# Pool branch by token in plain fp32 beside a modulation summed column by column

## The chip, the cores and the metric

The kernel runs on one core of one Trainium2 chip. The metric is the device time of one execution in microseconds (us). Its engines are TensorE (PE; its weight loads are PEld), VectorE (DVE), ScalarE (ACT), GpSimd (POOL) and SyncE (SP), which issues nearly all transfers. They run beside each other and are held together by semaphores only.

## The reference

Three blocks work on `x`, 256 tokens by 2048 channels. Only the first is touched, and of it the modulation and the first half of the pooling mixer:

```python
m = jnp.dot(jax.nn.silu(c), w) + b              # c: 2048, w: 2048 x 6144
shift, scale, gate = jnp.split(m, 3, axis=-1)
h = rms_norm(x) * (1.0 + scale) + shift
u, g = jnp.split(h @ w_in, 2, axis=-1)          # w_in: 2048 x 4096
# four groups of 512 channels, windows 2, 4, 8, 16
pooled = stack([centred_window_mean(ug[:, :, i], w) - ug[:, :, i] for i, w in enumerate(POOL_WINDOWS)])
y = einsum('btgc,gcd->btgd', pooled, w_grp).reshape(B, T, BRANCH_W) * scale_p
x = x + gate * ((y * silu(g)) @ w_out)
```

A gated deltanet block (A), an attention block (B) and a last norm follow. The program reads 290 MB of weights once. Since `pooled` is a difference of means over tokens, the shift, which is the same at every token, drops out of it; only `g` needs it.

## The kernel before

**Split products.** Nearly all weights come as *pieces* of 128 x 1024 floats (512 KB, two tiles of 128 rows of k by 512 columns; the code calls one a slab) through `raw`, a ring of 4 slots. ACT rounds a piece into `w_hi` (`hi_parts`, L912), DVE takes the rest into `w_lo` (`lo_parts`, L1204), both rings of 8 slots, and PE makes three fp32r products for each tile of k and each 128 channels (`by_channel`, L539, L541, L542), so 24 matmuls of 256 columns for a slab. The operand is split the same way, into `a_hi` and `a_lo` or `b_hi` and `b_lo`. Eight slabs make a `group` of 512 output channels. The groups of the pool block are u and g of four channel groups (0 to 7, 64 slabs), `w_grp` (8 slabs) and `w_out` (32 slabs). SP refills a slot of `raw` when the lo part, or the gate sum, of the piece before it is done (`piece`, L354). The waiting is in the order of the program.

**Modulation.** 32 transfers of 1 MB (`mod_ring`, 6 slots) hold 128 rows of k each of the shift and then the scale part of `w_mod`. DVE adds them up, each times a column of `silu_c`, into `mod_acc` (L1242, L1246), and PE sums `mod_acc` over the partitions (`mod_sums`, L589). The gate part comes as every third piece of the stream of u and g; DVE adds it (`add_gate`, L1183), and PE sums it after group 7.

**Norm.** ACT squares `x`, DVE adds the squares, PE sums them (`partition_sums`, L579), and ACT makes the root `r1` (L930, L932). DVE and ACT then make `a_hi` and `a_lo` (L1230, L921, L1214).

**Pooling.** DVE makes the window sums of each channel group by shifted adds (L1226, L1297), with ACT's copy of u as their input (L961).

The order within an engine is the order of the code. Everything from the group `w_grp` on is the same work before and after, with other line numbers.

Of the kernel before, what the change touches and what calls it, by code (L numbers as in the profile page):

```python
# [53 lines left out]
O_H, O_POOLED, O_Z = KT, KT + 4, KT + 8  # L54
# [9 lines left out]
V_C, V_BMOD, V_PSC, V_FG, V_NW0, V_NW1, V_CONV = 0, 16, 64, 80, 96, 112, 128  # L64
V_ONW, V_QNW, V_KNW, V_ALOG, V_DTB, V_EDGE, V_END = 320, 321, 322, 323, 339, 355, 419
# [69 lines left out]
def program(nc, weights, mod_w, x_t, vecs_d, consts_d, w_ab_d, bias_d, out_d):  # L135
    ctx = ExitStack()
    with ctx:
# [35 lines left out]
        r1 = at("r1", [P, T], F32)  # L173
# [3 lines left out]
        silu_c = at("silu_c", [P, KT], F32)  # L177
# [13 lines left out]

        mod_acc = at("mod_acc", [P, D], F32, t34_at)
# [63 lines left out]
        s_mod = [sem(f"s_mod{i}") for i in range(MOD_SLOTS)]  # L256
        s_mod_used = sem("s_mod_used")
        s_mod_sum = sem("s_mod_sum")
        s_vec = sem("s_vec")
        s_con = sem("s_con")  # L260
        s_x = sem("s_x")
        s_shift = sem("s_shift")
# [6 lines left out]
        s_act_read = sem("s_act_read")  # L269
        s_x1 = sem("s_x1")  # L270
        s_eps = sem("s_eps")
        s_pads = sem("s_pads")
# [72 lines left out]
        def _(sp):  # L345
            sp.dma_start(vecs[:], vecs_d).then_inc(s_vec, 16)
            for i in range(2 * KT):
                if i >= MOD_SLOTS:
                    sp.wait_ge(s_mod_used, i - MOD_SLOTS + 1)
                sp.dma_start(mod_ring[:, i % MOD_SLOTS], mod_w[i]).then_inc(s_mod[i % MOD_SLOTS], 16)  # L350
                if i == 1:
                    sp.dma_start(xres[:], x_t).then_inc(s_x, 16)

            def piece(q, slot, var=None, mul=0):  # L354


                before = q - RAW_SLOTS
                if before >= 0 or var is not None:
                    if before % 3 == 2:
                        sp.wait_ge(s_gate, Num(before // 3 + 1, var, mul // 3).v)  # L360
                    else:
                        sp.wait_ge(s_lo, Num(before // 3 * 2 + before % 3 + 1, var, mul // 3 * 2).v)
                land(Num(q, var, mul), slot)

            def land(q, slot):
                sp.dma_start(raw[:, slot], weights[bass.ds(q.times(P).v, P), :]).then_inc(s_raw[slot], 16)

            for q in range(12):
                piece(q, q % RAW_SLOTS)
            with sp.Fori(1, 8) as i:  # L370
                for q in range(12):
                    piece(q, q % RAW_SLOTS, i, 12)
            for q in range(12 * 8, 12 * 8 + 4):
                piece(q, q % RAW_SLOTS)
# [9 lines left out]
            slabs_between(N_GRP + 4, middle)  # L384
# [19 lines left out]
        def _(pool):  # L404
# [4 lines left out]
            pool.memset(t0[:], 0.0).then_inc(s_pads, 1)  # L409
# [122 lines left out]
        def _(pe):  # L532
# [51 lines left out]
            def mod_sums(pieces):  # L584

                for m in range(KT):

                    col = 512 * (m // (KT // pieces)) + m
                    last = nc.tensor.matmul(misc[:, col:col + 1], mod_acc[:, m * P:(m + 1) * P],  # L589
                                            ones[:, 0:1], start=True, stop=True)  # L590
                    if (m + 1) % (KT // pieces) == 0:
                        last.then_inc(s_mod_sum, 1)

            pe.wait_ge(s_con, 16)
            pe.wait_ge(s_sums, 1)
            partition_sums(t0, misc[:, 0:T])
            pe.wait_ge(s_mod_used, KT)
            pe.wait_ge(s_root, 1)
            mod_sums(1)
            pe.wait_ge(s_mod_used, 2 * KT)  # L600
            pe.wait_ge(s_shift, 1)
            mod_sums(4)


            group(None, Num(0), 0, 0, a_hi, a_lo, ready=lambda kt: kt + 1)
            group(None, Num(SLABS), 1, 0, a_hi, a_lo)
            with pe.Fori(1, 4) as i:
                for k in range(2):
                    group(Num(k - 1, i, 2), Num(k * SLABS, i, 2 * SLABS), k, 0, a_hi, a_lo)

            pe.wait_ge(s_gate, GATES)
            mod_sums(1)
            for j in range(4):
                group(Num(G_GRP + j - 1), Num(N_GRP + j * GRP_SLABS), j % 2, j * GRP_SLABS, b_hi, b_lo,
                      kt0=4 * j, slabs=GRP_SLABS, ready=lambda kt: O_H + j + 1)
# [8 lines left out]
            for j in range(4):  # L624
                g = Num(G_WOUT + j)
                group(g + (-1), slab_of(g), j % 2, N_WOUT % HL_SLOTS, a_hi, a_lo,
                      ready=lambda kt: O_POOLED + kt // 4 + 1, fillers={6: early_sums} if j == 3 else None)
# [270 lines left out]
        def _(act):  # L898
# [40 lines left out]
            for j, t in enumerate((t0, t1, t2, t1)):  # L939
                if j == 3:  # L940
                    act.wait_ge(s_dve, 1)
# [749 lines left out]
```

## Time and profile before

| | us |
|---|---|
| time, median of 3 runs (1568.35 to 1570.14) | 1568.76 |
| the profiled execution's own time | 1570.54 |
| its span | 1568.7 |
| PE busy | 1430.3 (91%) |
| DVE busy | 960.5 (61%) |
| ACT busy | 756.4 (48%) |
| moved by DMA | 302.56 MB, mean 193 GB/s |

Times within the profile are counted from the start of the span. A matmul's modelled end overlaps the next one's start: what one costs is the distance between two starts, not its "mean ns". The releaser of an idle stretch stands behind "<-".

### The profile page before, as it was taken

Reading aid. Unit: us, or ns where it says so; the run is one execution under the profiler, and the core shown is the slowest. Engines: PE = TensorE matmul, PEld = TensorE weight load, DVE = VectorE, ACT = ScalarE, POOL = GpSimd, SP = SyncE. Lnnn points to the kernel's source line nnn. Section 1 sums busy time; section 2 is a strip of 40 time slices with the busy share of each in tenths; the row PEclk is TensorE's granted clock in tenths of the full one; section 3 lists DMA queues with packets and bytes.
Section 4 is the critical chain, followed back from the end, with each engine's and each line's share of the span. In section 5 each row is a group of like instructions: output and inputs, shape, how many; then the busy total and the mean of one; then the engine's idle time right before and its main releaser. Section 6 shows DMA issues by size and latency. Waiting matters only on the chain.

```text
span 1568.7 us, 27728 instructions
## 1 busy us (share of the span) xinstructions
PE 1430.3 (91%) x11070; PEld 1398.6 (89%) x11070; DVE 960.5 (61%) x1092; ACT 756.4 (48%) x856; POOL 121.6 (8%) x128
## 2 busy tenths in 40 slices
PE   0149999999999999999959999999999999999998
PEld 0149999999999899899959999999999899998998
DVE  6798777776555666658863544674555655556542
ACT  2024444445557556573333555644656646556431
POOL 0000000000010212202033430000000000000000
PEclk9999999899999999999969999999999999999999
DMA  9977877765445444456474446655555655554562
GB/s 397 394 264 256 287 271 261 234 208 180 156 147 176 153 162 140 152 168 196 122 208 147 143 140 176 230 165 171 188 175 162 192 170 180 180 161 160 177 187 82
DMA packets 85500, 302.56 MB, mean 193 GB/s; under 512 B 17264, under 2 KB 17392, under 8 KB 80944
## 3 DMA queue, kind: packets, MB, share of 16 engines
q1 hardware_dynamic: 79584, 278.12, 53.7%
q0 software_dynamic: 5840, 23.33, 4.6%
q8 instruction: 59, 0.97, 0.3%
q14 instruction: 17, 0.14, 0.0%
HBM read 289.88 MB, written 13.63 MB: 193 GB/s over the span
## 4 chain that ended last, share of the span: by engine, by line
PE 46%; DVE 4%; ACT 1%; DMA 1%; issue 1%; SPq 0%; DVEq 0%; ACTq 0%
PE acc L539 11%; PE acc L541 11%; PE acc L542 11%; PE misc L737 2%; PE acc L550 2%; PE acc L552 2%; PE acc L551 2%; DVE w_lo L1204 1%; DVE t L1415 1%; DMA raw<-weights 1%; PE misc L854 0%; PE misc L788 0%; PE misc L831 0%; DVE prod L1226 0%; DVE inv L1226 0%
## 5 line engine op out<-in xcount | busy, mean ns | idle before, releaser
L1204 DVE TENSOR_TENSOR w_lo<-raw,w_hi 128x1024 fp32r<-128x1024 f32 x424 | 515.3, 1235 | 385.2 <-ACT w_hi L912 383.8
L912 ACT ACTIVATE w_hi<-raw 128x1024 fp32r<-128x1024 f32 x424 | 437.6, 1053 | 420.9 <-DMA raw<-weights 205.0
L539 PE MATMUL acc<-b_hi,w_hi 128*128 128x256 f32 x1856 | 534.8, 288 | 3.6 <-DVE w_lo L1204 3.5
L541 PE MATMUL acc<-b_lo,w_hi 128*128 128x256 f32 x1856 | 527.2, 284 | 0.0
L542 PE MATMUL acc<-b_hi,w_lo 128*128 128x256 f32 x1856 | 527.0, 284 | 0.0
L539 PE MATMUL acc<-a_hi,w_hi 128*128 128x256 f32 x1280 | 365.1, 285 | 2.5 <-DVE w_lo L1204 2.5
L541 PE MATMUL acc<-a_lo,w_hi 128*128 128x256 f32 x1280 | 364.1, 284 | 0.0
L542 PE MATMUL acc<-a_hi,w_lo 128*128 128x256 f32 x1280 | 364.0, 284 | 0.0
L539 PEld LDWEIGHTS acc<-b_hi,w_hi 128*128 128x128 f32 x1856 | 358.2, 193 | 4.8 <-DVE w_lo L1204 4.2
L541 PEld LDWEIGHTS acc<-b_lo,w_hi 128*128 128x128 f32 x1856 | 358.1, 193 | 0.6
L542 PEld LDWEIGHTS acc<-b_hi,w_lo 128*128 128x128 f32 x1856 | 357.7, 193 | 0.0
L539 PEld LDWEIGHTS acc<-a_hi,w_hi 128*128 128x128 f32 x1280 | 247.8, 194 | 2.8 <-DVE w_lo L1204 2.7
L541 PEld LDWEIGHTS acc<-a_lo,w_hi 128*128 128x128 f32 x1280 | 247.7, 194 | 0.1
L542 PEld LDWEIGHTS acc<-a_hi,w_lo 128*128 128x128 f32 x1280 | 247.7, 193 | 0.0
L589 PE MATMUL misc<-consts,mod_acc 128*128 128x1 f32 x96 | 18.6, 328 | 64.2 <-DVE mod_acc L1246 64.2
L1246 DVE SCALAR_TENSOR_TENSOR mod_acc<-mod_ring,silu_c,mod_acc 128x2048 f32<-128x2048 f32 x30 | 70.5, 2351 | 10.5 <-DMA mod_ring<-mod_w 7.3
L589 PEld LDWEIGHTS misc<-consts,mod_acc 128*128 128x128 f32 x96 | 18.5, 300 | 65.0 <-DVE mod_acc L1246 65.0
L737 PE MATMUL misc<-t,t 128*128 128x128 f32 x320 | 43.1, 296 | 15.1 <-POOL t L483 10.7
L737 PEld LDWEIGHTS misc<-t,t 128*128 128x128 f32 x320 | 41.7, 211 | 15.5 <-POOL t L483 10.9
L1415 DVE SCALAR_TENSOR_TENSOR t<-t,conv_now,t 128x255 f32<-128x255 f32 (+2 forms) x96 | 40.4, 494 | 16.8 <-ACT t L1021 16.8
L550 PE MATMUL acc<-w_hi,b_hi 128*128 128x512 f32 x128 | 50.3, 393 | 0.0
L552 PE MATMUL acc<-w_hi,b_lo 128*128 128x512 f32 x128 | 49.9, 390 | 0.0
(206 smaller groups left out, 1286.3 us busy)
## 6 DMA issues: line engine op xcount, KB each, us to landing
raw<-weights SPq DMA_DIRECT2D x456, 512.0 KB, 4.4
mod_ring<-mod_w SPq DMA_DIRECT2D x32, 1024.0 KB, 9.0
xres<-x_t SPq DMA_DIRECT2D x1, 2048.0 KB, 12.9
x_d<-xres POOLq DMA_DIRECT2D x1, 2048.0 KB, 7.7
l_d<-l_t POOLq DMA_DIRECT2D x4, 512.0 KB, 3.0
a_d<-a_t POOLq DMA_DIRECT2D x4, 512.0 KB, 3.0
l_x<-l_d POOLq DMA_DIRECT2D x4, 512.0 KB, 4.8
a_x<-a_d POOLq DMA_DIRECT2D x4, 512.0 KB, 4.1
```

The lines of the kernel that those rows point to most:

```text
L539: nc.tensor.matmul(to, wh[:, ch], xh, start=kt == 0 and m % 2 == 0, stop=False, skip_group_check=True)
L541: nc.tensor.matmul(to, wh[:, ch], xl, start=False, stop=False, skip_group_check=True)
L542: last = nc.tensor.matmul(to, wl[:, ch], xh, start=False, stop=end and m % 2 == 1, skip_group_check=True)
L550: nc.tensor.matmul(to, xh[:, t], wh, start=kt == 0, stop=False)
L551: nc.tensor.matmul(to, xh[:, t], wl, start=False, stop=False)
L552: last = nc.tensor.matmul(to, xl[:, t], wh, start=False, stop=end)
L589: last = nc.tensor.matmul(misc[:, col:col + 1], mod_acc[:, m * P:(m + 1) * P], ones[:, 0:1], start=True, stop=True)
L737: last = nc.tensor.matmul(misc[:, k:k + P], tile_of(lhs, half, h), tile_of(rhs, half, h), start=True, stop=True)
L912: nc.scalar.activation(w_hi[:, m.c % HL_SLOTS], raw[:, q.c % RAW_SLOTS], ACT.Copy).then_inc(own.up(s_hi), 1)
L1204: nc.vector.tensor_tensor(w_lo[:, slot], raw[:, q.c % RAW_SLOTS], w_hi[:, slot].bitcast(F32), ALU.subtract).then_inc(own.up(s_lo), 1)
L1246: ins = nc.vector.scalar_tensor_tensor(out=mod_acc[:], in0=mod_ring[:, i % MOD_SLOTS], scalar=silu_c[:, i % KT:i % KT + 1], in1=mod_acc[:] ...
L1415: ins = nc.vector.scalar_tensor_tensor(out=out, in0=src[:, m * T:(m + 1) * T - d], scalar=conv_now[:, 4 * m + 3 - d:4 * m + 4 - d], in1=ou ...
```

## The change

- **Modulation by columns.** `w_mod` is handed over transposed, 128 output columns on the partitions by 2048 of k. PE first spreads `c` over all partitions (4 products of 128x512), ACT takes silu of it (`silu_b`, 128x2048), and one `tensor_tensor_reduce` of DVE per transfer gives 128 finished values (`summed`, `mod_column`). There are 16 transfers for the scale and 16 for the shift, in an order written out by `scale_at` and `shift_at`, in a ring of 4 slots; the last four shift blocks go to two slots in `vo`. `mod_sums` is gone.
- **u by token.** `x * (1 + scale)` goes to `vo` (`modulated`, ACT). PE multiplies it by plain fp32 `w_in`, k outermost: for each of 16 tiles of k, 4 column groups by 2 halves of the tokens, one product 128x512 each, into all 8 banks of PSUM. The weights come through `u_ring` (8 slots of 512 KB, in the place of `w_lo`). The root of the norm is applied when ACT copies u out (`u_by_token`).
- **Pooling as products.** 8 fp32 products of 136 columns for each group with a constant `window` (`pool_windows`); ACT and DVE split the result into `b_hi` and `b_lo` from PSUM.
- **g** stays in split fp32r products: first the lower half of k for all four column groups, then the upper half, into four pairs of banks (`g_half`): 32 slabs instead of 64 for u and g.
- **Gate.** Its 32 pieces now stand between slabs 20 to 51 of the stream, one to a slab (before: one to two slabs of 64): in the last 12 slabs of g, the 8 of `w_grp` and 12 of `w_out`.

```diff
+MOD_SLOTS = 4
+U_SLOTS = 8
+N_GRP = 4 * SLABS
+N_GATE = 20
+MOD_SLOT = [i % 4 for i in range(26)] + [3, 1, 4, 5, 4, 5]
...
+            for kt in range(KT):                                     # SP
+                mod_block(scale_at(kt))
+                if kt < 4:
+                    sp.dma_start(xres[:, 4 * kt:4 * kt + 4], x_t[:, 4 * kt:4 * kt + 4]).then_inc(s_x[kt], 16)
+                u_piece(kt, 0)
+                if kt == 4:
+                    mod_block(shift_at(0))
+                    mod_block(shift_at(1))
+                u_piece(kt, 1)
+                if kt in (7, 9, 11, 13):
+                    mod_block(shift_at((kt - 7) // 2 + 2))
+                if kt in (12, 14):
+                    piece(kt - 12)
+                    piece(kt - 11)
...
+            for kt in range(4):                                      # PE
+                u_first(kt)
+                u_ready(kt, 1)
+                u_part(kt, 2)
+            row_sums()
+            u_first(4)
             pe.wait_ge(s_root, 1)
-            mod_sums(1)
+            for kt in range(4):
+                u_part(kt, 3).then_inc(s_u_used[1], 1)
+            u_ready(4, 1)
+            u_part(4, 2)
+            u_part(4, 3).then_inc(s_u_used[1], 1)
+            for kt in range(5, KT - 2):
+                u_first(kt)
+                u_ready(kt, 1)
+                u_part(kt, 2)
+                u_part(kt, 3).then_inc(s_u_used[1], 1)
...
+            def summed(tile, weight, col, start, out, done):         # DVE
+                nc.vector.tensor_tensor_reduce(out=tile, in0=tile, in1=weight, scale=1.0, scalar=start,
+                                               op0=ALU.mult, op1=ALU.add, accum_out=out
+                                               ).then_inc(own.up(done), 1)
...
                     nc.vector.tensor_tensor(w_lo[:, slot], raw[:, q.c % RAW_SLOTS],
                                                     w_hi[:, slot].bitcast(F32), ALU.subtract
                                                         ).then_inc(own.up(s_lo), 1)
+                    if m.var is None and N_GATE <= m.c < N_GATE + GATES:
+                        add_gate(m.c - N_GATE)
...
+            lo_parts(Num(0), 2)                                      # DVE, after the last scale column
+            shift_column(6)
+            normed(6)
+            lo_parts(Num(2), 2)
+            operand_a(6)
+            shift_column(7)
+            normed(7)
+            for kt in range(8, 12):
+                shift_column(kt)
+                operand_a(kt - 1)
+                normed(kt)
+            pooled_lo(0)
...
+            operand_a(11)                                            # ACT
+            hi_parts(Num(5), 1)
+            u_by_token(3)
...
-            for j, w in enumerate(WINDOWS):
-                add(dst[:, :, 0:reach], src[:, :, 0:reach], src[:, :, d:d + reach],
```

PE's queue from its start, before; `s_mod_used` is the count of DVE's sums, `s_hu` that of ACT's scaled tiles of x, `s_u0` to `s_u7` are the slots of `u_ring`:

```order
1 L579 MATMUL misc<-t_58,consts 128x256 [waits s_sums,s_con]
2 L579 MATMUL misc<-t_58,consts 128x256 x3
3 L589 MATMUL misc<-consts,mod_acc 128x1 [waits s_root,s_mod_used]
4 L589 MATMUL misc<-consts,mod_acc 128x1 x15
5 L589 MATMUL misc<-consts,mod_acc 128x1 [waits s_shift,s_mod_used]
6 L589 MATMUL misc<-consts,mod_acc 128x1 x15
7 L539 MATMUL acc<-a_hi,w_hi 128x256 [waits s_opnd,s_lo]
```

And of the change, up to the first tiles of column group 3:

```order
1 L734 MATMUL misc<-c_row,consts 128x512 [waits s_c,s_con]
2 L734 MATMUL misc<-c_row,consts 128x512 x3
3 L691 MATMUL acc<-u_ring,vo 128x512 [waits s_u0,s_hu]
4 L691 MATMUL acc<-u_ring,vo 128x512 x3
5 L691 MATMUL misc<-u_ring,vo 128x512 [waits s_u1]
6 L691 MATMUL misc<-u_ring,vo 128x512
...
19 L713 MATMUL misc<-consts,t_58 128x1 [waits s_sums]
20 L713 MATMUL misc<-consts,t_58 128x1 x7
21 L675 MATMUL misc<-t_58,consts 128x256 x4
22 L691 MATMUL acc<-u_ring,vo 128x512 [waits s_u0,s_hu]
23 L691 MATMUL acc<-u_ring,vo 128x512 x3
24 L691 MATMUL misc<-u_ring,vo 128x512 [waits s_root]
25 L691 MATMUL misc<-u_ring,vo 128x512 x7
```

PE now has its large products behind the first scale column instead of behind the last transfer; the sums of the squares stand between them.

DVE's queue in the stretch where gate pieces are in the stream, before (between two groups):

```order
75 L1183 SCALAR_TENSOR_TENSOR mod_acc<-raw,silu_c,mod_acc 128x1024 [waits s_gate,s_raw3]
76 L1204 TENSOR_TENSOR w_lo<-raw,w_hi 128x1024 [waits s_hi] x2
77 L1183 SCALAR_TENSOR_TENSOR mod_acc<-raw,silu_c,mod_acc 128x1024 [waits s_gate,s_raw2]
78 L1204 TENSOR_TENSOR w_lo<-raw,w_hi 128x1024 [waits s_hi] x2
```

And of the change (its lines L1403 are the sum over a row and the read-out of its result; L1432 is `w_lo`):

```order
114 L1432 TENSOR_TENSOR w_lo<-raw,w_hi 128x1024 [waits s_hi] x9
115 L1403 ISA raw,gate_half<-raw,silu_b,vecs 128x1024 [waits s_raw1]
116 L1403 ISA gate_half 128x1
117 L1432 TENSOR_TENSOR w_lo<-raw,w_hi 128x1024 [waits s_hi]
118 L1403 ISA raw,modv<-raw,silu_b,gate_half 128x1024 [waits s_gate,s_raw3]
119 L1403 ISA modv 128x1
```

A gate sum now follows every lo part instead of every second one.

## Rows read from the trace of the kernel before

**Rows 1.** Stretches: length, each engine's busy time (instructions), PEclk, DMA share, GB/s.

```profile
80.00:100.00 20.00, 0.00 (x0) 0.00 (x0) 18.74 (x9) 2.11 (x2) 0.00 (x0) 1.00 0.85 349
150.00:200.00 50.00, 50.00 (x419) 50.00 (x419) 37.21 (x35) 22.65 (x22) 0.00 (x0) 1.00 0.77 255
```

**Rows 2.** PE's waits, first 620 us: total, times, longest.

```profile
PE misc L589 <- DVE mod_acc L1246: 64.2, 2, 38.8
PE misc L579 <- DVE t L1226: 26.3, 1, 26.3
```

**Rows 3.** Timeline of the start: start, us, engine, line, what, count, idle before.

```profile
1.25 0.67 POOL L405 DMA_DIRECT2D consts<-consts  x1 [0.81 <-POOLq L1685]
...
26.27 3.75 PE L579 MATMUL misc<-t,consts 128*128 128x256 f32 x8 [26.27 <-DVE t L1226]
30.06 0.47 ACT L930 ACTIVATE r<-misc,small 128x256 f32<-128x256 f32 x1 [4.20 <-PE misc L579]
...
31.85 0.42 ACT L932 ACTIVATE r<-r 128x256 f32<-128x256 f32 x1
...
108.07 0.56 PE L539 MATMUL acc<-a_hi,w_hi 128*128 128x256 f32 x1
```

**Rows 4.** Transfers: the rate from 15 to 85 us; KB and us to landing of `consts`.

```profile
DMA packets 3875, 28.21 MB, mean 403 GB/s; under 512 B 432, under 2 KB 432, under 8 KB 432
...
consts<-consts POOLq DMA_DIRECT2D x1, 512.0 KB, 8.7
```

**Rows 5.** Groups over the whole span: count | busy us, mean ns | idle before.

```profile
L1246 DVE SCALAR_TENSOR_TENSOR mod_acc<-mod_ring,silu_c,mod_acc 128x2048 f32<-128x2048 f32 x30 | 70.5, 2351 | 10.5 <-DMA mod_ring<-mod_w 7.3 <-DVE mod_acc L1246 0.5
L1230 DVE SCALAR_TENSOR_TENSOR t<-xres,modv,r 128x256 f32<-128x256 f32 x16 | 6.7, 480 | 0.1
L1242 DVE TENSOR_SCALAR mod_acc<-mod_ring,silu_c 128x2048 f32<-128x2048 f32 x2 | 2.6, 1282 | 6.6 <-DMA mod_ring<-mod_w 6.6
L1149 ACT ACTIVATION_READ_ACCUMULATOR p_t<-p_t,row_max 128x1 f32 x32 | 6.0, 187 | 0.0
L1141 ACT ACTIVATE v_n<-acc,r_tok 128x512 f32<-128x512 f32 x8 | 5.1, 685 | 17.2 <-PE acc L552 17.2
L1045 ACT ACTIVATE dec_t<-misc 128x1536 f32<-128x1536 f32 x4 | 5.8, 1454 | 19.1 <-PE misc L646 19.1
```

**Rows 6.** Groups of the u and g stretch, 108 to 291 us.

```profile
L1204 DVE TENSOR_TENSOR w_lo<-raw,w_hi 128x1024 fp32r<-128x1024 f32 x61 | 74.0, 1223 | 38.3 <-ACT w_hi L912 37.7
L912 ACT ACTIVATE w_hi<-raw 128x1024 fp32r<-128x1024 f32 x62 | 65.7, 1059 | 92.6 <-DMA raw<-weights 92.4
```

**Rows 7.** Two gate sums of DVE; one more and four lo parts lie between.

```profile
178.78 1.28 DVE L1183 SCALAR_TENSOR_TENSOR mod_acc<-raw,silu_c,mod_acc 128x1024 f32<-128x1024 f32 x1
...
189.94 1.28 DVE L1183 SCALAR_TENSOR_TENSOR mod_acc<-raw,silu_c,mod_acc 128x1024 f32<-128x1024 f32 x1
```

**Rows 8.** The `raw` transfers' way from issue to landing, 110 to 292 us.

```profile
DMA to landing us min/median/max: 3.4/4.8/7.3
```

**Rows 9.** A run of plain fp32 products inside a group (two instructions a product).

```profile
1168.28 0.60 PE L854 MATMUL misc<-p_tt,v_n 128*128 128x256 f32 x2
...
1170.82 0.36 PE L539 MATMUL acc<-b_hi,w_hi 128*128 128x256 f32 x1
```

**Rows 10.** PE around the end of u and g, and fp32 alone at 806 us.

```profile
299.26 4.65 PE L589 MATMUL misc<-consts,mod_acc 128*128 128x1 f32 x32
303.77 0.56 PE L539 MATMUL acc<-b_hi,w_hi 128*128 128x256 f32 x1
...
308.40 0.32 PE L539 MATMUL acc<-b_hi,w_hi 128*128 128x256 f32 x1
...
806.75 3.70 PE L737 MATMUL misc<-t,t 128*128 128x128 f32 x16 [10.66 <-POOL t L483]
...
810.40 0.28 PE L541 MATMUL acc<-b_lo,w_hi 128*128 128x256 f32 x1
810.52 0.28 PE L542 MATMUL acc<-b_hi,w_lo 128*128 128x256 f32 x1
```

More of the change, by code:

```diff
@@ L345, in _ @@
         def _(sp):
+            sp.dma_start(c_row[:], c_d).then_inc(s_c, 16)
             sp.dma_start(vecs[:], vecs_d).then_inc(s_vec, 16)
[L347 to L354, printed above, removed]
-                before = q - RAW_SLOTS
[L358 to L374, printed above, removed]
+            def mod_block(i):
+                if 4 <= i < 28 or i >= 30:
+                    sp.wait_ge(s_mod_used, mod_before(i) + 1)
+                elif i >= 28:
+                    sp.wait_ge(s_pool, 2 if i == 28 else 4)
+                slot = MOD_SLOT[i]
+                to = mod_ring[:, slot] if slot < MOD_SLOTS else mod_late[:, slot - MOD_SLOTS]
+                sp.dma_start(to, mod_w[i]).then_inc(s_mod[slot], 16)
@@ new lines, in u_part, with u_ready @@
+            def u_part(kt, j):
+                for half in range(2):
+                    last = nc.tensor.matmul(bank(2 * j + half), vo[:, kt, half * P:(half + 1) * P],
+                                            u_ring[:, 2 * (kt % 4) + j // 2, j % 2 * GC:(j % 2 + 1) * GC],
+                                            start=kt == 0, stop=kt == KT - 1, skip_group_check=True)
+                return last
+            def u_ready(kt, half):
+                pe.wait_ge(s_u[2 * (kt % 4) + half], 16 * (kt // 4 + 1))
@@ new lines, in u_first, with row_sums @@
+            def u_first(kt):
+                pe.wait_ge(s_hu, kt + 1)
+                u_ready(kt, 0)
+                u_part(kt, 0)
+                u_part(kt, 1).then_inc(s_u_used[0], 1)
+            def row_sums():
+                pe.wait_ge(s_sums, 1)
+                for half in range(2):
+                    for k in range(4):
+                        at_ = 2 * GC + T + half
+                        nc.tensor.matmul(misc[:, at_:at_ + 1], t0[:, k * T + half * P:k * T + (half + 1) * P],
+                                         ones[:, 0:1], start=k == 0, stop=k == 3)
+                partition_sums(t0, misc[:, 2 * GC:2 * GC + T])
@@ new lines, in pool_windows @@
+            def pool_windows(j):
+                if j == 0:
+                    pe.wait_ge(s_window, 16)
+                pe.wait_ge(s_utok, j + 1)
+                out = pair_of_banks(j)
+                for m in range(GM):
+                    ch = slice(m * P, (m + 1) * P)
+                    nc.tensor.matmul(out[:, m * T:m * T + REACH], u_tok[:, j, 0, ch], window[:, j, 0],
+                                     start=m % 2 == 0, stop=False, skip_group_check=True)
+                    last = nc.tensor.matmul(out[:, (m + 1) * T - REACH:(m + 1) * T], u_tok[:, j, 1, ch],
+                                            window[:, j, 1], start=False, stop=m % 2 == 1, skip_group_check=True)
+                last.then_inc(s_pool, 1)
```

505 lines of the change are left out of this document (315 added, 190 removed).

## The prediction

> **What bounds the kernel now.** I read the stretches first, then PE's waits, then the timeline of the start. Once PE has begun on u and g it doesn't stop: 419 matmuls in 50 us, one every 0.119 us [rows 1], so 2.86 us for a slab of 24. Until then it is nearly empty: it starts on u and g at 108.07 us [rows 3], and before that it waits 64.2 us for DVE's modulation sums and 26.3 us for the squares [rows 2]. What lies under this wait is the transfer of 32 MB (349 GB/s in the stretch 80 to 100 us [rows 1], 403 from 15 to 85 us [rows 4]). So two things can make this kernel shorter: less work for PE behind the start, or work for it inside the empty 108 us. The change does both for u. It takes 64 - 32 = 32 slabs out, 32 x 2.86 = 91.5 us of PE, and gives PE plain fp32 products while the modulation arrives. The question is when g can begin, and whether the stream of weights then keeps up with PE.
>
> All times are against the profiled execution (1570.54 us; its span is 1568.7). The point of comparison is the first slab of `w_grp`: now at 303.77 us, with PE at half pace until 308.40 [rows 10], which costs 2.3 us more, so 306.1 as if at full pace. Behind it the work is the same.
>
> **Prices.** A plain fp32 run of 4 products of 256 and 4 of 128 columns takes 1170.82 - 1168.28 = 2.54 us for 1536 columns [rows 9], 1.65 ns a column, 0.85 us for 512. At the start PE is at the lower of its two clocks, 1.2 GHz: 4 products of 256 columns take 3.75 us, end included [rows 3], 3.7 ns a column. Of DVE, lo part 1.22, 128x256 operation 0.48; of ACT, hi part 1.06, 128x512 from PSUM 0.69 [rows 5, 6]. The sum over a row with read-out doesn't occur before. The nearest row is the three-operand form on 128x2048 at 2.35 us; ACT's read of an accumulator is 0.19 [rows 5]. So 2.35 to 2.54, I take 2.45, and for a gate piece 1.28 + 0.19 = 1.47.
>
> **Step 1, to the first u product.** `consts` is issued at 1.25 and lands 8.7 us later [rows 3, 4], at 9.95; PE now waits for it with all that follows. Spreading c: 4 x 512 columns at 3.7 ns is 7.5 us, to 17.5. Silu of 128x2048 by ACT: 1454 ns for 1536 columns from PSUM [rows 5], so 1.9, to 19.4. First column sum 2.45, scaled tile 0.5: 22.3 us. Before, DVE's first sum needs only its own transfer; now it stands behind all this, and only the filling of the rings goes on meanwhile.
>
> **Step 2, to the fifth tile of k.** 24 products for tiles 0 to 3 are 20.4 us, plus 2.3 for a start at the lower clock (as at 303.77): 45.0. Sums of squares: 16 one-column instructions at 4.5/32 = 0.14 us [rows 10] and 4 x 256 columns, 4.0: 49.0. The first half of tile 4 is 3.4 (it hides ACT's root, 32.27 - 30.06 = 2.2 us [rows 3]): 52.4, and the first tile of column group 3 1.7: 54.1. Only then is a slot of the second half of `u_ring` free, and SP, which is in order, has stood at it with all modulation blocks queued behind. The transfers issued by then (about 14 MB, 35 us) are long done: some 15 us of DMA time are lost.
>
> **Step 3, the transfers.** From 54.1 there are 0.5 MB, 11 tiles of 2.1 MB, 4 shift blocks of 1.05 and 4 pieces of g: 29.9 MB, 74.2 us at 403 GB/s, with 0.35 for the issue and 3.4 - 1.3 = 2.1 of fixed landing time [rows 8]: 130.7 for the last u weights, 128.1 for the last scale block, 131 for its scaled tile. PE alone would be through 9 of those tiles (6.8 each) at about 124, so here the transfers decide, by little. At 349 GB/s [rows 1] it would be 142.
>
> **Step 4, from the last scale column to g.** DVE, from 130.5: 4 lo parts 4.9, 6 shift columns 14.7, 6 + 5 operations of 0.48 are 5.3: 155.4. ACT then has `a_hi` of tile 11, one hi part and `u_by_token(3)`, 0.5 + 1.06 + 1.37 = 2.9: 158.3. `pool_windows(3)`, 8 x 136 columns, 1.8: g starts at **160**. PE alone would be done at 131 + 13.6 + 5.4 = 150, so DVE's chain decides. PE is idle for some 8 us before and falls to the lower clock: 2.3 us again. DVE's window sums are gone, but they lay beside PE's matmuls: nothing for them in the sum.
>
> **Step 5, g.** 768 matmuls x 0.1193 = 91.6: from 160.1 + 2.3 to 254.0. Against 306.1 that is 52.1 us earlier.
>
> **Step 6, gate pieces.** In the 32 slabs from the 21st on, two pieces now go through 4 slots for 2.86 us of PE. In u and g ACT waited 92.4 us for weights and never for PE [rows 6], so the loop of slots set the pace of the lo parts: 6 pieces in 189.94 - 178.78 = 11.2 us, 1.86 each [rows 7], 3.72 for two. If a slot took only 3.4 us to land [rows 8] plus issue, hi and lo, two slabs would take 6.0, 3.0 each. A gate piece needs no ACT, so between: 3.4. The lo part of slab 11 comes late, behind the last four shift columns of DVE, at about 186; slab 20's is ready at 202.7 where PE wants it at 219.6, 16.9 us of lead. Slabs 20 to 40 use 21 x (3.4 - 2.86) = 11.3 of it. In the `w_grp` stretch DVE has 2 x 1.22 + 2 x 1.47 + 4 x 0.48 + 1.22 = 8.5 us for 5.7 of PE, four times: 11.2. Three more gate slabs: 1.6. 11.3 + 11.2 + 1.6 - 16.9 = **7 us lost** (0 at 3.0, 15 at 3.72).
>
> **Sum.** 1570.5 - 52.1 + 7.2 = 1525.6. The profiled execution is 1.8 us above the median of the runs, so **1524**.
>
> **Two rules of the Trainium skill that speak against it.** PE rises to the higher clock in plain fp32 work: after 10.66 us idle 16 instructions of 128 columns take 3.4 us, twice the high-clock price, and right behind them matmuls start 0.12 apart [rows 10]. The Trainium skill (TensorE: Matmul & The Clock Gate, HAM oscillation) says that a loop which waits for a transfer at each tile of k falls to the low clock on each of them. By that rule the first rival below would come true; by the row it would not while tiles of 6.8 us wait for under a microsecond. And three-operand work on two fp32 sources takes 2.35 us where one source takes 1.28 [rows 5], the lower rate already. The Trainium skill (Vector Engine (DVE) Microarchitecture Reference, Points that are easy to get wrong) says that with two such sources both read ports are used and none is left for reading back the accumulator. If that meant another halving, the second rival would hold; no row shows it.
>
> **Rivals.** *u at 1.2 GHz (slower).* If PE stays at the lower clock through u, 128 products cost 1.7 us instead of 0.85: 22 + 218 + 4 + 7 = 251 instead of 160, 91 us more, 1615. For it: PE's start is at that clock [rows 3]. Against it: at 1.7 us a product PE never waits in this stage, and dense fp32 work was seen to raise the clock [rows 10]. It turns the sign from about 1.33 us a product on. 6%.
>
> *The sum over a row at half rate (none, or slightly slower).* At 4.8 us a column DVE needs 22 x 4.8 + 9.5 from 19.4, 134.5 for the last scale column (4 later); six shift columns 14 more; g starts at 178. A gate slab costs DVE 1.22 + 2.6 = 3.8 us: 21 x 1.0 against a lead of only 7.5, the `w_grp` stretch 20, three slabs 3: 37 lost instead of 7. 1524 + 18 + 30 = 1572. 8%.
>
> *The stream keeps up and PE decides.* Transfers somewhat above 403 GB/s or an earlier start, no loss in step 6: g at 150, 1524 - 10 - 7 = 1507. That is the lower part of my own case.
>
> *It doesn't hide.* 16.8 MB of u weights now share the DMA with the modulation. If the transfers of the stage ran at the 255 GB/s of u and g [rows 1], step 3 would take 117 us, 43 more, 1567: no measurable change. Against it, that rate was asked for by 4 slots; here 12 larger ones stand ready. 3%.
>
> **How the numbers follow.** My case has 83%; its own range is 1502 (PE decides, no loss, `c` spread partly at the higher clock, 5) to 1543 (349 GB/s, 11.5, and 8 more in step 6). The range of 8 in 10 is 1498 to 1556, a little wider than that for stalls of a few us that low clock doubles; the slow rivals lie outside it. What a measurement can tell from no change here is 0.2%, 3 us. Faster 0.85 (my case and part of the doubtful rest), same 0.05, slower 0.10.
>
> **What would show it.** Right: the first fp32 u product at 22, u weights landing until 131, products 0.85 us apart, a first g matmul at 160 and `w_grp` at 254; a stall of several us behind lo parts in slabs 40 to 52. Wrong: a column sum over 3 us; u products 1.7 us apart after the first; gaps in g itself behind `a_lo`; PE waiting behind gates already in slabs 25 to 35, which would mean a slot loop above 4 us.

## The result and the profile after

| | before | after |
|---|---|---|
| time, median of 4 runs each (us) | 1568.67 (1568.35 to 1570.14) | 1532.05 (1530.91 to 1534.7) |
| span of the profiled execution | 1568.7 | 1532.7 |

The ratio is 0.9767, with a 95% interval of 0.975 to 0.9784: the kernel is 36.6 us faster. I had predicted 1524, in a range of 1498 to 1556. The time is 8 us above the forecast, and the size of the gain stands on two errors of opposite sign, which the traces show.

First the page of after: busy time, share of the span, instructions; and the groups of the new operations (count | busy us, mean ns | idle before).

```profile
PE 1447.7 (94%) x10550; PEld 1347.5 (88%) x10550; DVE 907.4 (59%) x1089; ACT 734.1 (48%) x844; POOL 120.1 (8%) x128
...
L1403 DVE CUSTOM_DVE_ANT_0 mod_ring<-mod_ring,silu_b,vecs 128x2048 f32<-128x2048 f32 x28 | 65.6, 2350 | 64.8 <-DMA mod_ring<-mod_w 51.2
L691 PE MATMUL acc<-u_ring,vo 128*128 128x512 f32 x128 | 61.6, 628 | 10.0 <-ACT vo L1114 10.0
```

PE's busy share is 94% now. The sum over a row takes 2350 ns where the three-operand form took 2351 [rows 5], and its read-out, an instruction of its own, 0.08 us (below).

The timeline of the start and of the passage from u to g, in the same columns as [rows 3]:

```profile
8.13 7.19 PE L734 MATMUL misc<-c_row,consts 1*128 1x512 f32 x8 [8.13 <-DMA consts<-consts]
...
15.35 1.88 ACT L1153 ACTIVATE silu_b<-misc 128x2048 f32<-128x2048 f32 x1 [13.34 <-PE misc L734]
17.26 2.35 DVE L1403 CUSTOM_DVE_ANT_0 mod_ring<-mod_ring,silu_b,vecs 128x2048 f32<-128x2048 f32 x1 [13.50 <-ACT silu_b L1153]
19.54 0.08 DVE L1403 DVE_READ_ACCUMULATOR2_ANT modv<- 128x1 f32 x1
...
20.27 6.11 PE L691 MATMUL acc<-u_ring,vo 128*128 128x512 f32 x8 [4.96 <-ACT vo L1114]
26.23 1.88 PE L691 MATMUL misc<-u_ring,vo 128*128 128x512 f32 x4
27.94 2.31 PE L691 MATMUL acc<-u_ring,vo 128*128 128x512 f32 x5
...
127.87 8.66 PE L691 MATMUL acc<-u_ring,vo 128*128 128x512 f32 x16 [4.48 <-ACT vo L1114]
...
154.06 0.82 PE L725 MATMUL misc<-window,u_tok 128*128 128x136 f32 x2 [4.95 <-ACT u_tok L1134]
...
157.70 0.57 PE L635 MATMUL acc<-a_hi,w_hi 128*128 128x256 f32 x1
```

A 128x512 product is two instructions. The first ones stand 0.86 us apart; the four of the row at 26.23 reach to 27.94, 0.43 us apart, 0.86 for a product, as the prediction had it. That the first ones ran at the lower clock is read from this spacing alone: the clock column reads 1.00 for the stretch 20 to 25 us too. PE works on u from 20.27 us on instead of waiting until 108.07 [rows 3], and g starts at 157.70.

SP's queue and the transfers: the wait of SP with the longest single stretch in the first 160 us (total, times, longest), and the stretches with their DMA share and GB/s in the last two columns, as in [rows 1].

```profile
SPq L421 <- PE misc L691: 35.9, 9, 24.5
```

```profile
40.00:60.00 20.00, 20.00 (x64) 10.68 (x63) 3.63 (x3) 2.18 (x3) 0.54 (x1) 1.00 0.43 159
60.00:120.00 60.00, 59.48 (x139) 26.14 (x138) 35.67 (x40) 9.42 (x18) 0.00 (x0) 1.00 1.02 416
```

SP stands 24.5 us at the second half of u's fifth tile, until 52.25; around it the transfers fall to 159 GB/s. Behind it they run at 416 GB/s until the last modulation is there.

Then the end of g. PE's waits in the whole first 330 us (total, times, longest), and the stretches behind 250 us, of which columns 3 and the last three count (PE busy, clock, DMA share, GB/s):

```profile
PE acc L635 <- DVEq L1566: 16.9, 3, 13.0
PE acc L691 <- ACT vo L1114: 10.0, 3, 5.0
PE misc L734 <- DMA consts<-consts: 8.1, 1, 8.1
PE misc L725 <- ACT u_tok L1134: 4.9, 1, 4.9
```

```profile
160.00:250.00 90.00, 90.00 (x753) 90.00 (x752) 63.62 (x73) 33.89 (x35) 0.00 (x0) 1.00 0.82 278
...
260.00:280.00 20.00, 7.04 (x48) 6.83 (x48) 16.61 (x23) 7.24 (x8) 0.00 (x0) 0.66 0.84 290
280.00:300.00 20.00, 16.09 (x109) 15.69 (x109) 17.20 (x28) 6.65 (x7) 0.00 (x0) 0.83 0.76 247
```

g itself has no gap. But a new wait of 16.9 us stands behind it, with the clock down to 0.66 of full speed in one stretch. L1566 is DVE's release of a pair of banks behind `z(j)`, the product of group j of `w_grp` with its gate branch. The first product of `w_grp` and the one behind the longest wait, then DVE's queue at that place:

```profile
250.21 0.28 PE L635 MATMUL acc<-b_hi,w_hi 128*128 128x256 f32 x1
...
274.85 0.58 PE L635 MATMUL acc<-b_hi,w_hi 128*128 128x256 f32 x1 [12.96 <-DVEq L1566]
```

```profile
269.55 1.22 DVE L1432 TENSOR_TENSOR w_lo<-raw,w_hi 128x1024 fp32r<-128x1024 f32 x1 [0.29 <-ACT w_hi L1087]
270.69 1.28 DVE L1403 CUSTOM_DVE_ANT_0 raw<-raw,silu_b,vecs 128x1024 f32<-128x1024 f32 x1
271.90 0.08 DVE L1403 DVE_READ_ACCUMULATOR2_ANT gate_half<- 128x1 f32 x1
271.90 0.17 DVE L1456 TENSOR_TENSOR gains<-vecs 128x16 f32<-128x16 f32 x1
271.99 1.65 DVE L1460 SCALAR_TENSOR_TENSOR t<-acc,vecs,vo 128x256 f32<-128x256 f32 x4
274.76 1.22 DVE L1442 TENSOR_TENSOR a_lo<-t,a_hi 128x1024 fp32r<-128x1024 f32 x1 [1.12 <-ACT a_hi L1094]
...
280.59 1.66 DVE L1460 SCALAR_TENSOR_TENSOR t<-acc,vecs,vo 128x256 f32<-128x256 f32 x4
```

`z(0)` (L1460) stands behind the lo part and the gate sum of slab 40. `w_grp` has four groups of two slabs in two pairs of banks, so the third group, at slab 36, needs the banks that `z(0)` gives back. PE wanted them at 261.9 and got them at 274.85. The lo parts, on which I had kept my eyes, were there. `z(1)` follows 8.60 us behind `z(0)`, nearly all of it work of DVE (one wait of 1.12 us), where PE takes 5.7 for the two slabs between: the two later waits, 1.3 and 2.6 us, come from that.

**The account.** `w_grp` starts at 250.21; the point of comparison was 306.1, so 55.9 us were gained up to there. 36.0 are left in the span. So 19.9 were lost behind 250 us. Nearer to the cause the loss is larger: the first product of block A starts at 424.56 before and at 390.45 now, so 21.8 us are lost up to there, and the rest, which is the same work, was 1.9 shorter in this execution. Of the 21.8, 16.9 are the waits. 42 matmuls behind the first and the last of them (until 277.6, and from 292.05 to 298.2) stand 0.21 us apart instead of 0.12, which is some 4 more. I had predicted 52.1 gained and 7 lost.

### The profile page after: what moved, and what is told of

Same layout as the page of the kernel before. It is cut to its first block, busy times and chain, and to the rows that moved or that the text cites. A ratio compares the mean times of both kernels' runs of the same rounds, so it can differ in the third digit from the quotient of the medians.

```text
span 1532.7 us, 26253 instructions
## 1 busy us (share of the span) xinstructions
PE 1447.7 (94%) x10550; PEld 1347.5 (88%) x10550; DVE 907.4 (59%) x1089; ACT 734.1 (48%) x844; POOL 120.1 (8%) x128
## 4 chain that ended last, share of the span: by engine, by line
PE 47%; DVE 2%; ACT 1%; issue 1%; DMA 0%; SPq 0%; DVEq 0%; ACTq 0%
PE acc L635 12%; PE acc L637 12%; PE acc L638 12%; PE misc L916 2%; PE acc L647 2%; PE acc L646 2%; PE acc L648 2%; DVE t L1653 1%; DVE w_lo L1432 1%; PE misc L1033 0%; PE misc L967 0%; PE misc L1010 0%; DMA raw<-weights 0%; PE misc L960 0%; DVE vo L1460 0%
## 5 line engine op out<-in xcount | busy, mean ns | idle before, releaser
L1432 DVE TENSOR_TENSOR w_lo<-raw,w_hi 128x1024 fp32r<-128x1024 f32 x392 | 480.1, 1244 | 364.9 <-ACT w_hi L1087 363.8
L635 PE MATMUL acc<-b_hi,w_hi 128*128 128x256 f32 x1856 | 534.6, 288 | 17.9 <-DVEq L1566 14.3
L635 PEld LDWEIGHTS acc<-b_hi,w_hi 128*128 128x128 f32 x1856 | 358.1, 193 | 19.5 <-DVEq L1566 14.7
L635 PE MATMUL acc<-a_hi,w_hi 128*128 128x256 f32 x896 | 255.9, 286 | 2.6 <-DVEq L1566 2.6
L637 PE MATMUL acc<-a_lo,w_hi 128*128 128x256 f32 x896 | 254.9, 284 | 0.0
L638 PE MATMUL acc<-a_hi,w_lo 128*128 128x256 f32 x896 | 254.8, 284 | 0.0
L635 PEld LDWEIGHTS acc<-a_hi,w_hi 128*128 128x128 f32 x896 | 173.5, 194 | 2.9 <-DVEq L1566 2.8
L637 PEld LDWEIGHTS acc<-a_lo,w_hi 128*128 128x128 f32 x896 | 173.5, 194 | 0.1
L638 PEld LDWEIGHTS acc<-a_hi,w_lo 128*128 128x128 f32 x896 | 173.4, 193 | 0.0
L1403 DVE CUSTOM_DVE_ANT_0 mod_ring<-mod_ring,silu_b,vecs 128x2048 f32<-128x2048 f32 x28 | 65.6, 2350 | 64.8 <-DMA mod_ring<-mod_w 51.2
L691 PE MATMUL acc<-u_ring,vo 128*128 128x512 f32 x128 | 61.6, 628 | 10.0 <-ACT vo L1114 10.0
L691 PE MATMUL misc<-u_ring,vo 128*128 128x512 f32 x128 | 57.5, 592 | 0.0
L916 PE MATMUL misc<-t,t 128*128 128x128 f32 x320 | 41.7, 289 | 14.6 <-POOL t L579 10.3
L1653 DVE SCALAR_TENSOR_TENSOR t<-t,conv_now,t 128x255 f32<-128x255 f32 (+2 forms) x96 | 40.4, 494 | 16.9 <-ACT t L1246 16.9
```

What stands on the lines that cost most here:

```text
L635: nc.tensor.matmul(to, wh[:, ch], xh, start=kt == 0 and m % 2 == 0, stop=False, skip_group_check=True)
L637: nc.tensor.matmul(to, wh[:, ch], xl, start=False, stop=False, skip_group_check=True)
L638: last = nc.tensor.matmul(to, wl[:, ch], xh, start=False, stop=end and m % 2 == 1, skip_group_check=True)
L691: last = nc.tensor.matmul(bank(2 * j + half), vo[:, kt, half * P:(half + 1) * P], u_ring[:, 2 * (kt % 4) + j // 2, j % 2 * GC:(j % 2 + 1) ...
L916: last = nc.tensor.matmul(misc[:, k:k + P], tile_of(lhs, half, h), tile_of(rhs, half, h), start=True, stop=True)
L1403: nc.vector.tensor_tensor_reduce(out=tile, in0=tile, in1=weight, scale=1.0, scalar=start, op0=ALU.mult, op1=ALU.add, accum_out=out).then_i ...
```

## The experiments

Theory: the loss behind 250 us comes from where `z(0)` stands in DVE's queue, with the gate pieces in front of it; the start is a chain in which SP's wait at the fifth tile and PE's wait for `consts` count fully. Each time is a median, with the ratio to the kernel before on the same chip. No run takes the parts of the change (modulation by columns, u by token, pooling as products) back one at a time, so what each gained up to `w_grp` is read from the timeline and not shown by a run.

### z two and four slabs earlier on DVE

```diff
-            lo_parts(Num(12), N_GRP - 3)
+            lo_parts(Num(12), N_GRP - 3 - 2)          # and - 4
...
-                lo_parts(Num(N_GRP + 9 + 2 * j), 2)   # behind each z(j)
+                lo_parts(Num(N_GRP + 9 - 2 + 2 * j), 2)
```

ACT's rounding of z follows two slabs earlier in both.

> The same with half the distance: z after the lo parts of slab 38, 40, 42, 44. Theory A: each slab that z(0) is moved ahead is worth the price of one slab of DVE's stream with its gate sum, 2.7 to 3.3 us, so 5 to 7 us: 1525 to 1527. Theory B: 1529 to 1532.

> Only the order of DVE and ACT behind g is changed: the products with silu(g) (z) of the four groups of w_grp stand after the lo parts of slab 36, 38, 40, 42 instead of 40, 42, 44, 46, and the rest of the lo parts follow. Theory A (the 13.0 us wait of PE at 274.85 is for a bank that z(0) frees, and z(0) stands in DVE's queue behind the lo parts and gate sums of slabs 37 to 40): in the changed kernel z(0) began at 271.99; the lo part of slab 36 was done about 11 to 12 us earlier, so the first wait nearly goes, the two later ones (1.33 and 2.58) shrink or stay, and of the 16.9 us of waits plus about 4 at the lower clock some 13 to 17 go: 1516 to 1519. Theory B (the stream of weights is what is late; the bank only happens to be named): the waits come back behind w_lo within the next ten slabs and the time moves by less than 5 us, 1528 to 1532.

Two slabs: 1526.62, ratio 0.9735 (0.9719 to 0.9751), as expected; the first wait for L1566 fell from 13.0 to 6.0 us, and one of 2.9 for a lo part came new. Four slabs: 1540.54, ratio 0.9825 (0.9808 to 0.9841), 8.5 us slower than the change where I had expected 13 to 16 us less. DVE's and ACT's queues in that run:

```profile
255.99 1.65 DVE L1460 SCALAR_TENSOR_TENSOR t<-acc,vecs,vo 128x256 f32<-128x256 f32 x4
261.79 1.23 DVE L1442 TENSOR_TENSOR a_lo<-t,a_hi 128x1024 fp32r<-128x1024 f32 x1 [4.15 <-ACT a_hi L1094]
```

```profile
258.85 1.06 ACT L1087 ACTIVATE w_hi<-raw 128x1024 fp32r<-128x1024 f32 x1 [1.79 <-DMA raw<-weights]
259.81 1.01 ACT L1150 ACTIVATE vo<-misc 128x1024 f32<-128x1024 f32 x1
260.71 1.05 ACT L1094 ACTIVATE a_hi<-t 128x1024 fp32r<-128x1024 f32 x1
267.72 1.06 ACT L1087 ACTIVATE w_hi<-raw 128x1024 fp32r<-128x1024 f32 x1 [5.96 <-DMA raw<-weights]
```

`z(0)` is made at 256, in time. But ACT's rounding of it stands behind the hi part of slab 38, which waits for its transfer, and behind the last gate branch (L1150), and DVE stands 4.15 us at `a_lo` for the rounding, with the lo parts and gate sums behind it that would free the slots for the next transfers. So ACT then waits 5.96 us. This circle turned once for each z, about 12 us for two slabs of which PE takes 5.7.

### z four slabs earlier on both engines

```diff
-                hi_parts(Num(27 + 4 * j), 4 if j < 3 else 2)
+                hi_parts(Num(27 + 4 * j), (4, 4, 2, 0)[j])
...
-                hi_parts(Num(N_GRP + 9 + 2 * j), 2)
+                hi_parts(Num(N_GRP + 9 - 4 + 2 * j), 2)
```

> z(j) stands four slabs earlier in DVE's queue as in the run that moved it by four, but the rounding on ACT is moved by four too, so that it no longer stands behind the hi part of slab 38. If the 4.2 to 4.5 us that a_lo waited for a_hi each time were why that run lost, they go, PE's waits in this stage fall below 8 us, and the time is 1516 to 1522. Rival: DVE and the slots are simply short of time in the w_grp stretch, lo parts come late instead, and it is no better than moving z by two: 1526 or more.

1527.95, ratio 0.9736 (0.9718 to 0.9754): about 13 us better than with ACT's order as it was, so the circle was why that run lost. But it is no better than moving z by two, as the rival said. PE's waits behind 250 us are spread now, and more than half of them are for lo parts:

```profile
PE acc L635 <- DVE w_lo L1432: 5.8, 7, 2.8
...
PE acc L635 <- DVEq L1566: 3.8, 2, 2.6
```

So the place of z is only part of it. The z's stand 8.60 us apart in this run too (258.07, 266.67, 275.27), against 5.7 of PE: with a gate sum behind each lo part DVE is short of time in this stage wherever z stands.

### No gate pieces

All gate pieces are left out (the gate is then `b_mod` alone), SP's stream is the weights only.

> The gate part of the modulation is left out: its 32 transfers and its 32 sums are gone, the gate is the bias alone. Everything else is as in the change. Theory A and B alike: DVE and the slots keep up with PE, the lead grows to the 8 slots and PE's 16.9 us of waits and its two drops of the clock between 260 and 300 us go. Then 1532 - 20 = 1512. If it stays above 1525, the waits there have another cause (the order of z alone, or ACT's silu of g), and step 6 of the prediction named the wrong thing.

1511.8, ratio 0.9642 (0.9625 to 0.9658), as expected. That is 20.2 us less than the change, and the account above has 19.9 lost behind 250 us. From the start of `w_grp` to the first product of block A this run takes 118.65 us, before it was 118.5 from the point of comparison, in the change 140.2: the whole loss is the gate pieces'. PE doesn't wait in that stage at all, with z where the change has it, and the z's are 6.2 us apart.

### Gate pieces eight slabs earlier

```diff
-N_GATE = 20
+N_GATE = 12
```

> The gate pieces go with slabs 12 to 43 instead of 20 to 51. If the loss behind 262 us comes only from where z(0) stands in DVE's queue, the first wait for it (13.0 us) stays, since ACT found 8 slabs of lead at 259 in the change's trace, and the two later waits (1.3 and 2.6 us, with the low clock they bring) go because only three gate slabs are left behind z(0): about 1528. Rival, by the loop of slots as I had it in step 6 (3.4 us for a slab with a gate piece against 2.86): 8 more gate slabs lie ahead of z(0), it comes 4.3 us later, and the sum is 1532 to 1537.

1544.62, ratio 0.984 (0.9816 to 0.9863): the rival, and more of it than I gave it. The lo parts of DVE in two stretches, first of the change, then without gate pieces, then here (columns: stretch, length, busy (instructions), clock, DMA share, GB/s):

```profile
190.00:200.00 10.00, 7.29 (x6) 1.00 0.93 300
200.00:250.00 50.00, 17.04 (x14) 1.00 0.88 292
```

```profile
200.00:250.00 50.00, 22.06 (x18) 1.00 0.62 199
```

```profile
190.00:200.00 10.00, 3.68 (x3) 1.00 0.83 302
200.00:250.00 50.00, 17.39 (x15) 1.00 0.90 304
```

With a gate piece for each, 14 or 15 slabs come in 50 us, one in 3.3 to 3.6 us, where PE takes 2.86; without, 18, as fast as PE takes them. The change builds its lead between 190 and 200, where six lo parts are made; with `N_GATE = 12` only three are, the lead is never built, `z(0)` comes at 283.96 instead of 271.99, and PE's first wait for it is 18.5 us. My expectation rested on a misread row of the change's trace, ACT's hi part of slab 37:

```profile
259.04 1.06 ACT L1087 ACTIVATE w_hi<-raw 128x1024 fp32r<-128x1024 f32 x1 [3.39 <-PE acc L638]
```

The view names PE, which I took for a ring of eight slots that was full. It wasn't. `w_grp` starts with slab 32 at 250.21, so at 259 PE was at slab 35, two ahead of which ACT worked; the slot that slab 37 needs had been free since PE was done with slab 29, at 244.5. SP issued the transfer of this slab at 254.44, and it took 4.6 us to land, until 259.0: ACT had waited for it, as in nearly all other rows of that stage.

### SP's order at the fifth tile

```diff
-            for kt in range(KT):
+            for kt in (0, 1, 2, 3, 4, *range(8, KT)):
...
+                    for k in (5, 6, 7):               # behind shift_at(1), before u_piece(4, 1)
+                        mod_block(scale_at(k))
+                        u_piece(k, 0)
+                    for k in (4, 5, 6):
+                        u_piece(k, 1)
```

> Only the order of SP's transfers is changed: three scale blocks and the first halves of u tiles 5 to 7 go ahead of the second half of tile 4, on which SP stood for 24.5 us. Theory A (between 35 and 52 us the DMA is idle only because SP is in order, and the late transfers of tiles 14 and 15 then hold PE up for 4.5 us at 127.87): 4.7 MB, 11 us of transfers, move into the idle time; PE ends the u products 4 to 5 us earlier, DVE's chain behind the last scale column starts up to 11 us earlier but then waits for PE's slots of u_ring, and g starts 3 to 7 us earlier than 157.7: 1525 to 1529. Rival: what is gained at the start of g is given back at the bank of z(0), since DVE's stream is then no earlier: 1531 to 1532.

1524.04, ratio 0.9721 (0.9705 to 0.9737), 8.0 us better than the change. The stretches of this run:

```profile
40.00:60.00 20.00, 20.00 (x64) 10.56 (x63) 10.47 (x12) 4.50 (x8) 0.54 (x1) 1.00 0.90 336
60.00:120.00 60.00, 60.00 (x141) 26.60 (x140) 33.20 (x34) 9.51 (x16) 0.00 (x0) 1.00 1.01 411
```

The hole of 159 GB/s is filled to 336, and g starts at 148.46 instead of 157.70.

### A row of ones of its own

`c` is spread with a row of ones that GpSimd fills, not with one that comes with `consts`.

```diff
+            pool.memset(ones_row[:], 1.0).then_inc(s_row, 1)
...
-            pe.wait_ge(s_con, 16)
+            pe.wait_ge(s_row, 1)
```

> c is spread from a row of ones that GpSimd fills, so PE no longer waits for consts (8.13 us in the change's trace). c itself is issued at 0.74, 0.41 us ahead of vecs, which has landed at 3.58, so the spreading can start at about 3.2, 4.9 us earlier. If the start is a chain (spread, silu, column sum, scaled tile, u products of tiles 0 to 3, only then the ninth u slot), all 4.9 us go through to the end: first u product at 15.4, g at 152.8, about 1527. Rival: the first blocks of modulation and the transfers behind them decide, and the gain is under 1 us: 1531 to 1532.

1525.96, ratio 0.9727 (0.9706 to 0.9748), 6.1 us better; g starts at 151.30, 6.4 earlier. PE now waits 2.6 us, for `c` itself. Nearly all of it goes through to the end.

### Each scale column summed twice

The second sum runs over the product of the first, so the scales come out as other numbers; only the time is of use.

```diff
+                summed(tile, silu_b[:], ..., s_twice)  # before the sum of mod_column, in scale_column
```

> Each of the 16 scale columns is summed twice (the second time over the product of the first, so the scales are other numbers): 16 x 2.35 = 37.6 us more work for DVE, which in the change's trace is busy 52 of the 102 us from 25 to 127. If transfers and PE set the pace of that stage, only the first sum (2.35) and the last (2.35) lie on the path: g starts at 160 to 163 instead of 157.7, and the time is 1535 to 1538. Rival: the column sums are on the path all along, and the time is about 1565.

1537.58, ratio 0.9798 (0.9779 to 0.9818), 5.5 us more; g starts at 162.37, 4.7 later. DVE's busy time from 25 to 127 us rose from 51.82 to 84.25 us, and nearly all of it lay beside transfers. So in this stage DVE's sums are on the path only at its two ends, as step 3 had it.

### Slots of their own for the gate pieces

The pieces go to `t0` and `t1`, not through `raw`, and stand behind the lo parts of slabs 12 to 40.

```diff
+                sp.dma_start((t0, t1)[k % 2][:, 0:D // 2], weights[row:row + P, :]).then_inc(s_raw_gate[k % 2], 16)
```

> The gate pieces no longer pass the four slots of the weights: they have two of their own (t0, free behind the window products, and t1, free until z(0)), and stand behind the lo parts of slabs 12 to 40 (two behind 20, 24 and 28), z where it was. If the cause is that a gate piece in the ring makes each slab 3.5 to 3.6 us (lo parts of slabs 20 and 32 end at 199.9 and 243.3 in the change's trace) and so brings z(0) to 272 instead of before 261, then lo parts keep the full lead of 8 slabs, z(0) comes at about 256 as without gate pieces, the waits behind 262 go, and the time is that of the run without them: 1512 to 1515. Rival: the bytes are the cause (1.05 MB a slab is 2.6 us at 403 GB/s, and both kinds land later side by side), and it stays at 1525 or more.

1539.15, ratio 0.9805 (0.9786 to 0.9824), where 1512 to 1515 was expected: a miss by some 25 us, and 7 us slower than the change. DVE's waits in the trace, 160 to 345 us:

```profile
DVE w_lo L1433 <- ACT w_hi L1088: 22.7, 14, 3.0
DVE t L1404 <- DMA t<-weights: 22.6, 23, 2.0
```

DVE now waited 22.6 us for gate pieces. SP's queue is in order: a gate piece is issued only when DVE has done the one two before it, and the weights' pieces stand behind it. Against the run with the pieces in the ring from slab 12 on as well, 5.5 us were gained (the intervals of the two ratios overlap a little), but from 200 to 250 us the transfers moved only 316 GB/s.

### All three, and a third gate slot

With these two slots, SP's order and the row of ones together, and then with `t2` as a third slot:

```diff
-                sp.dma_start((t0, t1)[k % 2][:, 0:D // 2], ...
+                sp.dma_start((t0, t1, t2)[k % 3][:, 0:D // 2], ...
```

> Slots of their own for the gate pieces, SP's order at the fifth tile (8.0 us gained alone) and the row of ones (6.1 us gained alone) in one kernel. If the three act at different places, the sum is 1532 - 18 - 8 - 6 = 1500. Rival: the transfers of the start are the common limit of the last two (398 GB/s from 25 to 127 us with SP's order alone), so the row of ones adds nothing there: 1506. Rival of another kind, if slots of their own don't help: 1518 or more.

> As the run with all three edits and two gate slots, with a third gate slot (t2, free behind operand_a(15)). In the run with two slots DVE waited 22.6 us for gate pieces: one turn of a slot (issue, 4.8 us to land, the sum 1.36) is some 6.3 us, over two slots 3.15 us a slab, and slabs came at 3.1 to 3.2 us where PE takes 2.86. If the turn of the slots is the limit, three slots make it 2.1, the lo parts keep up, and the time falls from 1530 to 1500 to 1506. Rival: the transfers themselves are the limit: with the engines 0.91 busy they moved only 316 GB/s in this stretch, and 1.05 MB at 316 to 345 GB/s is 3.0 to 3.3 us a slab; then the third slot only lengthens the landings and the time stays at 1525 to 1531.

Two slots: 1529.97, ratio 0.9745 (0.9729 to 0.9762), a miss by 30 us of the 1500 expected, which had counted 18 us for the two slots of their own. Three: 1513.45, ratio 0.9649 (0.9633 to 0.9666), the fastest that computes everything, 18.6 us below the change. The stretch 180 to 230 us with two slots, and with three:

```profile
180.00:230.00 50.00, 44.41 (x354) 43.80 (x353) 33.99 (x43) 17.03 (x16) 0.00 (x0) 0.97 0.89 306
```

```profile
180.00:230.00 50.00, 50.00 (x419) 50.00 (x419) 44.33 (x58) 21.15 (x20) 0.00 (x0) 1.00 1.01 395
```

306 GB/s was not what the transfers can do: one more slot made it 395, at a DMA share of 1.01 instead of 0.89. Landing became slower (median 6.1 us for both kinds in this stretch, against 5.4 for gate pieces and 5.6 for the weights' with two slots), the rate higher. DVE's waits for gate pieces fell from 26.1 to 6.3 us. So the rival fell. But the full gain did not come either: `z(0)` is made at 256.75, and PE still waits 7.8 us for it. The prediction for this run, 1500 to 1506, missed by 7 us or more: it took the slots for the only limit; 1.05 MB at 395 GB/s is 2.65 us for a slab, little under PE's 2.86, so the lead isn't rebuilt. This last step is argued from the rates and wasn't tried by itself.

### The three edits with gate pieces in the ring

> The three edits that each gained alone, gate pieces left in the ring as in the change: SP's order at the fifth tile, the row of ones, and z two slabs earlier. With the first two together g started at 145.1 against 157.7 in the change (12.6 earlier; 9.2 by SP's order alone), and z two slabs earlier gained 5.4: 1532.0 - 12.6 - 5.4 = 1514. Rival: with g earlier, slab 20 finds less lead, so the gain of z is eaten by slabs of 3.5 us: 1518 to 1522.

1518.74, ratio 0.9678 (0.9662 to 0.9695), 13.3 us below the change, where the sum of the single gains is 19.5 and the forecast was 18. g starts at 144.84, as expected (12.9 earlier). A part is missing at the start already: alone, the two edits moved g by 9.2 and 6.4 us, 15.6 together. The rest is behind g:

```profile
PE acc L645 <- DVEq L1577: 11.2, 2, 8.7
...
PE acc L645 <- DVE w_lo L1443: 3.1, 1, 3.1
```

With z two slabs earlier alone these were 8.6 and 2.9. So 2.8 us more of waits: a part of what the start gains is given back here, where slabs come at the pace of the slots and not at PE's; that is the rival's story, and its time (1518 to 1522) came.

## Why the prediction was right, point by point

**The first u product** came at 20.27 (predicted 22.3): `consts` landed at 8.13, not 9.95; spreading, silu and sum took about what I had given them. That the half-rate rival fell shows in one row, 2.35 us and a read-out of 0.08. The Trainium skill (Vector Engine (DVE) Microarchitecture Reference, Points that are easy to get wrong) says that no read port is left for the accumulator beside two fp32 sources; here the read-out is a separate, short instruction, and it costs the sum nothing.

**u at the lower clock** fell too: products are 0.86 us from 25.4 us on, and PE hardly waited in the stage (59.48 of 60 us busy from 60 to 120). The one long wait, 4.48 us for the tiles of k 14 and 15, did cost clock: behind it 16 instructions took 8.66 us against 6.9 at full pace (granted clock 0.83 from 127 to 137 us), and behind the next, 4.95 us at 154.06, the window products and the first matmuls of g ran slowly too (0.59 from 150 to 158). The Trainium skill (TensorE: Matmul & The Clock Gate, HAM oscillation) speaks of a loop that waits at each tile of k and falls to the low clock each time; such a loop didn't come about here, and where PE waited once the trace agrees with the page.

**SP's fifth tile** was released at 52.25 (predicted 54.1), and its price is measured: I had some 15 us of transfers lost, and another order of SP gives back 9.2 us at the start of g, 8.0 at the end.

**The transfers** decided the stage. They ran at 416 GB/s against my 403, and the last scale block was there at 124.91, where I had 128.1. DVE had waited 4.68 us for it. The run with doubled sums shows that DVE did not decide there.

**g** started at 157.70 (predicted 160), behind a wait of 4.95 us for DVE's and ACT's chain where I had some 8, and took 92.5 us (predicted 93.9). Up to `w_grp` the forecast was 3.8 us too careful.

**The gate pieces** are the step that was mis-sized: 7 us predicted (0 to 15), 19.9 measured, and 20.2 by the run without them, outside my own bounds. The pace in it was nearly right: 14 lo parts in 50 us are 3.57 us a slab against my 3.4. That slab 40's lo part ended at 270.8, where I had 202.7 + 20 x 3.4 = 270.7, is luck: slab 20's was 2.8 us earlier than I had it, at 199.9, and the slower pace used that up. The 8.5 us of DVE for each z were right too (8.60). Wrong was the deadline. I measured the lead at slab 40, against PE's wish for slab 40, 276.8 in my numbers. But the queue of DVE holds `z(0)` behind slab 40, and PE wants its banks at slab 36, 11.4 us earlier. I had listed z's operations among DVE's work and asked only whether DVE keeps up, not where each of them is due. By my own numbers (an estimate) slab 40's gate sum and `z(0)` end at 270.7 + 1.5 + 1.9 = 274.1 where PE wants the banks at 265.4, 8.7 us of wait, and the two next waits are 8.5 - 5.7 = 2.8 each: 14.3 instead of 7. Measured were 13.0, 1.3 and 2.6, the first of them while the lead of the lo parts was still positive.

**The sum.** 1525.6 was forecast for the profiled execution: its span would be 1.8 less, 1523.8, and 1532.7 was measured, 8.9 more: 3.8 better up to `w_grp`, and 19.9 - 7.2 = 12.7 worse behind it. So the time came near the forecast, and inside the range, with help from the start: without these 3.8 us it would have been 12 off. Further on PE's waits are those of before (10.3 us where 10.7 were, 9.2 and 8.2 as before).

## What to carry to other kernels

When work is added to an in-order queue, a lead counted in the main item of that queue is not the lead of what stands between those items. For every consumer, write down where in the queue its item stands and when it is due; the earliest due one decides. And an operation that is moved earlier on one engine must be moved on each engine that it passes through, or the circle between them closes at the slowest place.

A transfer rate read under a ring of a few slots is the ring's rate. Before calling transfers the limit, ask how many can be under way, and whether an in-order issuer stands between them.

A releaser that a view names isn't always what was waited for. At 259.04 it named PE, whose slot had been free for some 15 us, and it was the transfer. Before an argument rests on such a name, work out from the program which slab stands there and when its slot was free.

## What the runs showed of the hardware

- The sum over a row of a product (`tensor_tensor_reduce`, fp32, 128x2048) takes 2350 ns, and its read-out is an instruction of its own of 0.08 us; 128x1024 takes 1.28 us. The three-operand form without the sum takes 2351 ns and 1.28 us [rows 5, 7], so the sum costs only its read-out.
- With pieces of 512 KB in four slots the DMA engines showed a busy share of 0.88 at 292 GB/s (the change, 200 to 250 us), with two more slots 0.89 at 306, with three more 1.01 at 395 (both 180 to 230). A busy share near 0.9 did not mean that there was nothing left.
- Plain fp32 products of 128x512 run as two instructions of 0.43 us each at the full clock and 0.86 at the lower one. Single waits of 4.5 and 5.0 us in a dense stretch were each followed by some us at the lower pace.
